# Recurrent scan of a hybrid decoder: sample states read once for both operands, output matmuls in runs of one shape, sample state update by four heads

## The reference, cut to what matters

```python
def _wkv_step(S, inp):
    r_t, w_t, k_t, v_t, a_t, b_t = inp
    sa = jnp.einsum('bhij,bhj->bhi', S, a_t)
    S = S * w_t[:, :, None, :] + sa[..., None] * b_t[:, :, None, :] + v_t[..., None] * k_t[:, :, None, :]
    return S, jnp.einsum('bhij,bhj->bhi', S, r_t)
```

## Time and profile before

| | |
|---|---|
| time, median of 3 runs | 3170.84 us (3169.41 to 3178.54) |
| profiled execution: span from first to last instruction | 3169.1 us |
| PE busy | 2695.0 us (85%), 21151 matmul passes |
| DVE, ACT, POOL busy | 1607.7, 1070.8, 174.8 us |
| first scan, from chunk 1 to the last state update | 258.19 to 455.70 us |
| second scan, the same | 2646.62 to 2839.11 us |

### The profile page before, as it was taken

The page is one execution under the profiler, slowest core; times in us unless marked ns, Lnnn a source line. Parts: engine busy times, 40 slices in busy tenths (PEclk is TensorE's granted clock), DMA queues, the critical chain, the costliest instruction groups (busy, mean ns, idle before and its releaser), DMA issues. The chain is left out here.

```text
span 3169.1 us, 48791 instructions
## 1 busy us (share of the span) xinstructions
PE 2695.0 (85%) x21151; PEld 2385.4 (75%) x21151; DVE 1607.7 (51%) x2358; ACT 1070.8 (34%) x1798; POOL 174.8 (6%) x176
## 2 busy tenths in 40 slices
PE   6939985998847899979989888978997939985999
PEld 5728854998724678869989866678997718864999
DVE  5384336644362577756434843265536374326643
ACT  4333112433311344434334620044434332203442
POOL 0020011000000000000000132200000020011000
PEclk8969867999865899989999965589998978967999
DMA  4210001444200222214434301323442210001442
GB/s 152 90 66 3 6 28 60 153 147 159 98 0 0 67 67 67 67 54 157 149 124 146 138 27 63 131 99 120 147 147 104 83 40 30 6 27 53 147 151 105
DMA packets 44133, 275.70 MB, mean 87 GB/s; under 512 B 5216, under 2 KB 5248, under 8 KB 14096
## 3 DMA queue, kind: packets, MB, share of 16 engines
q1 hardware_dynamic: 43680, 271.95, 24.1%
q0 software_dynamic: 240, 0.64, 0.1%
HBM read 256.32 MB, written 16.24 MB: 86 GB/s over the span
## 5 line engine op out<-in xcount | busy, mean ns | idle before, releaser
L315 PE MATMUL banks<-rounded,rounded 128*128 128x320 f32 x3184 | 1009.8, 317 | 165.3 <-DVE rounded L331 69.1
L316 PE MATMUL banks<-rounded,rounded 128*128 128x320 f32 x3184 | 995.7, 313 | 0.0
L317 PE MATMUL banks<-rounded,rounded 128*128 128x320 f32 x3184 | 995.2, 313 | 0.0
L305 DVE TENSOR_TENSOR rounded<-weight_ring,rounded 128x1024 fp32r<-128x1024 f32 x398 | 487.2, 1228 | 513.4 <-ACT rounded L298 513.1
L315 PEld LDWEIGHTS banks<-rounded,rounded 128*128 128x128 f32 x3184 | 609.4, 191 | 177.3 <-DVE rounded L331 74.3
L316 PEld LDWEIGHTS banks<-rounded,rounded 128*128 128x128 f32 x3184 | 609.7, 191 | 3.6
L317 PEld LDWEIGHTS banks<-rounded,rounded 128*128 128x128 f32 x3184 | 608.8, 191 | 0.0
L298 ACT ACTIVATE rounded<-weight_ring 128x1024 fp32r<-128x1024 f32 x398 | 419.2, 1058 | 414.6 <-PE banks L317 360.1
L942 PE MATMUL banks<-arena 64*64 64x64 f32 x4032 | 146.3, 225 | 22.8 <-PEq L788 20.3
L942 PEld LDWEIGHTS banks<-arena 64*64 64x64 f32 x4032 | 134.4, 140 | 31.0 <-issue 29.2
L470 ACT ACTIVATE arena<-banks 128x320 f32<-128x320 f32 x128 | 56.0, 438 | 247.9 <-PE banks L317 247.9
(11 more groups left out here) (361 smaller groups left out, 3593.1 us busy)
## 6 DMA issues: line engine op xcount, KB each, us to landing
weight_ring<-in_panels SPq DMA_DIRECT2D x206, 1024.0 KB, 4.7
arena<-in_pages SPq DMA_DIRECT2D x64, 320.0 KB, 3.4
arena<-in_ssm SPq DMA_DIRECT2D x8, 1024.0 KB, 4.8
out_ssm_sample<-arena SPq DMA_DIRECT2D x8, 1024.0 KB, 3.8
arena<-in_wkv SPq DMA_DIRECT2D x2, 2048.0 KB, 8.2
out_wkv_sample<-arena SPq DMA_DIRECT2D x2, 2048.0 KB, 6.2
consts<-in_consts SPq DMA_DIRECT2D x1, 1673.5 KB, 9.7
residual<-in_x SPq DMA_DIRECT2D x1, 1280.0 KB, 5.6
```

The lines of the kernel that those rows point to most:

```text
L305: self.k.nc.vector.tensor_tensor(self.k.w_lo[:, i % SPLIT], self.raw(i), self.k.w_hi[:, i % SPLIT].bitcast(F32), ALU.subtract)\
L315: mm(out, hi, x_hi, start=start, stop=False)
L316: mm(out, hi, x_lo, start=False, stop=False)
L317: return mm(out, lo, x_hi, start=False, stop=stop)
```

## The change

It edits `stage_rwkv_scan` alone.

- Sample chunk, xs: a product of a state now takes the sequence's 8 "a" and 8 "r" columns together (16 columns, written as two pieces of 8 with `pair`), and the two heads of a tile f alternate. ACT copies all 512 columns of the bank to `SX`. In x0 and y the state's part is then one product with the unit matrix for each head.
- x0 and y: all products of one kind for eight heads, then all of the other kind, where they took turns by head. Only the first product of a bank half starts with `start`.
- Sample state update: POOL multiplies the end columns by the decay before (`ends`, 16 operations at the start of the stage, read by the sample chunk's transposes) and multiplies SS by the decay when xs has read it (`SSp`, eight operations). The masks are made on DVE by four heads (`masks_of`, eight tensor_scalar of 256 columns each) into two buffers; DVE's multiply behind each add is gone, and so are POOL's masks.

```diff
@@ -908,8 +908,11 @@
-    zmask = [k.at(o, NB, CK), k.at(o + 512, NB, CK)]
+    zm = [k.at(RW["TMP"] + 2048 * i, NB, 4, CK) for i in range(2)]
+    ends = k.at(o, KT, P)
+    SX = [k.at(RW["TMP"] + 16 * P + 1792 * g + 512, 4, P) for g in range(2)]
...
+    pair = lambda a: a.rearrange("p (m t) -> p m t", m=2)
@@ -964,8 +968,11 @@
+                    if smp:
+                        pe.wait_ge(*pool_did.at("ends"))
                     for f in range(4 * g, 4 * g + 4):
-                        ins = nc.tensor.transpose(k.ps[:, 4 * g, (f % 4) * P:(f % 4 + 1) * P], BK[:, f * NCK + c, :], k.const("ident"))
+                        src = ends[:, f, :] if smp else BK[:, f * NCK + c, :]
+                        ins = nc.tensor.transpose(k.ps[:, 4 * g, (f % 4) * P:(f % 4 + 1) * P], src, k.const("ident"))
@@ -1006,10 +1013,11 @@
-                        for h, f, q, r in heads[g]:
+                        for f in range(4 * g, 4 * g + 4):
                             for b in range(NB):
-                                ins = mm(b3(g, 0)[r, q, TS * b:TS * b + TS], SS[r, f * NB + b, :],
-                                         AR[r, f * NCK + c, TS * b:TS * b + TS], start=True, stop=True)
+                                for r in half:
+                                    ins = mm(pair(k.ps[r, 4 * g, (f % 4) * P:(f % 4 + 1) * P])[:, :, TS * b:TS * b + TS], SS[r, f * NB + b, :],
+                                             pair(AR[r, f * NCK + c, :])[:, :, TS * b:TS * b + TS], start=True, stop=True)
                         ins.then_inc(*pe_did.tick("xs", c, g))
@@ -1018,10 +1026,11 @@
                         if smp:
-                            mm(b3(g, 3)[r, q, :], YM[g][r, q, :], eye[r, :], start=True, stop=False)
+                            mm(b3(g, 3)[r, q, :], SX[g][r, q, 0:CK], eye[r, :], start=q == 0, stop=False, skip_group_check=True)
                         elif c:
-                            mm(b3(g, 3)[r, q, :], AR[r, f * NCK + c, 0:CK], S[r, f, :], start=True, stop=False)
-                        ins = mm(b3(g, 3)[r, q, :], att[r, h, 0:CK], z[r, h, :], start=c == 0, stop=True)
+                            mm(b3(g, 3)[r, q, :], AR[r, f * NCK + c, 0:CK], S[r, f, :], start=q == 0, stop=False, skip_group_check=True)
+                    for h, f, q, r in heads[g]:
+                        ins = mm(b3(g, 3)[r, q, :], att[r, h, 0:CK], z[r, h, :], start=c == 0 and q == 0, stop=True, skip_group_check=True)
@@ -1036,24 +1045,22 @@
                     for h, f, q, r in heads[g]:
-                        ins = mm(b3(g, 3)[r, q, :], z[:, h, :], att[:, h, CK:P], start=True, stop=c == 0 or smp)
-                        if smp:
...
+                        ins = mm(b3(g, 3)[r, q, :], z[:, h, :], att[:, h, CK:P], start=q == 0, stop=c == 0, skip_group_check=True)
+                    if c:
+                        for h, f, q, r in heads[g]:
+                            lhs, rhs = (eye[r, :], SX[g][r, q, CK:P]) if smp else (S[r, f, :], AR[r, f * NCK + c, CK:P])
+                            ins = mm(b3(g, 3)[r, q, :], lhs, rhs, start=False, stop=True, skip_group_check=True)
                     ins.then_inc(*pe_did.tick("y", c, g))
...
+            for u in range(4):
+                pe.wait_ge(*vec_did.at("zm", u))
+                for f in (2 * u, 2 * u + 1):
+                    if f >= 4:
                         pe.wait_ge(*vec_did.at("SS", f - 4))
+                    for par in range(2):
+                        ins = mm(k.ps[half[par], f % 4, :], bktok[:, f, half[par]], zm[u % 2][:, :, 2 * (f % 2) + par, :],
+                                 start=True, stop=True)
+                ins.then_inc(*pe_did.tick("dss", u))
@@ -1086,7 +1093,7 @@
-                        s.activation(YM[g], b3(g, 0)[:, 0:4, :], ACT.Copy).then_inc(*act_did.tick("xs", c, g))
+                        s.activation(SX[g].rearrange("p a b -> p (a b)"), k.ps[:, 4 * g, :], ACT.Copy).then_inc(*act_did.tick("xs", c, g))
@@ -1159,27 +1166,38 @@
             vec.wait_ge(*pe_did.at("y", SMP, 1))
...
+            vec.wait_ge(*pool_did.at("SSp"))
+
+            def masks_of(u):
+                if u >= 2:
+                    vec.wait_ge(*pe_did.at("dss", u - 2))
+                for b in range(NB):
+                    ins = v.tensor_scalar(zm[u % 2][:, b, :, :], z[:, 4 * u:4 * u + 4, :], k.const("seq")[:, b:b + 1], None, ALU.mult)
+                ins.then_inc(*vec_did.tick("zm", u))
+
+            masks_of(0)
+            for u in range(4):
+                if u + 1 < 4:
+                    masks_of(u + 1)
+                vec.wait_ge(*pe_did.at("dss", u))
+                for f in (2 * u, 2 * u + 1):
+                    sf = SS[:, f * NB:(f + 1) * NB, :]
+                    v.tensor_tensor(sf, sf, k.ps[:, f % 4, :].rearrange("p (a b) -> p a b", a=NB), ALU.add).then_inc(*vec_did.tick("SS", f))
...
+            for m in range(2):
+                src = BK[:, SMP::NCK, m * CK:(m + 1) * CK].rearrange("p f (b t) -> p f b t", b=NB)
+                dst = ends[:, :, m * CK:(m + 1) * CK].rearrange("p f (b t) -> p f b t", b=NB)
+                for f in range(KT):
+                    ins = nc.gpsimd.tensor_tensor(dst[:, f], src[:, f], bc(pc[:, f, 4:12], TS), ALU.mult)
+            ins.then_inc(*pool_did.tick("ends"))
+            for g in range(2):
+                pool.wait_ge(*pe_did.at("xs", SMP, g))
+                for f in range(4 * g, 4 * g + 4):
+                    sf = SS[:, f * NB:(f + 1) * NB, :]
+                    ins = nc.gpsimd.tensor_tensor(sf, sf, bc(pc[:, f, 4:12], CK), ALU.mult)
+            ins.then_inc(*pool_did.tick("SSp"))
```

More of the change, by code:

```diff
@@ L910, in stage_rwkv_scan @@
         o += 1792
-    zmask = [k.at(o, NB, CK), k.at(o + 512, NB, CK)]
-    assert o + 1024 <= k.arena_size - 104, o
+    assert o <= k.arena_size - 104, o
+    zm = [k.at(RW["TMP"] + 2048 * i, NB, 4, CK) for i in range(2)]
+    ends = k.at(o, KT, P)
+    SX = [k.at(RW["TMP"] + 16 * P + 1792 * g + 512, 4, P) for g in range(2)]
+    assert o + KT * P <= k.arena_size - 104, o
     z = k.normed[:, 0:1024].rearrange("p (a b) -> p a b", a=16)
@@ L1038, in _ @@
                     for h, f, q, r in heads[g]:
-                        ins = mm(b3(g, 3)[r, q, :], z[:, h, :], att[:, h, CK:P], start=True, stop=c == 0 or smp)
-                        if smp:
[L1041 to L1046, removed]
+                        ins = mm(b3(g, 3)[r, q, :], z[:, h, :], att[:, h, CK:P], start=q == 0, stop=c == 0, skip_group_check=True)
[3 more added lines that the diff above has]
+                            ins = mm(b3(g, 3)[r, q, :], lhs, rhs, start=False, stop=True, skip_group_check=True)
                     ins.then_inc(*pe_did.tick("y", c, g))
             pe.wait_ge(*act_did.at("y", SMP, 0))
[L1049 to L1053, removed]
+            for u in range(4):
+                pe.wait_ge(*vec_did.at("zm", u))
+                for f in (2 * u, 2 * u + 1):
+                    if f >= 4:
                         pe.wait_ge(*vec_did.at("SS", f - 4))
-                    mm(k.ps[r, f % 4, :], bktok[:, f, r], zmask[par].rearrange("p a b -> p (a b)"), start=True, stop=True)\
-                        .then_inc(*pe_did.tick("dss", h))
+                    for par in range(2):
+                        ins = mm(k.ps[half[par], f % 4, :], bktok[:, f, half[par]], zm[u % 2][:, :, 2 * (f % 2) + par, :],
+                                 start=True, stop=True)
+                ins.then_inc(*pe_did.tick("dss", u))
         @block.scalar
```

## The result

The changed kernel takes 3034.32 us in the median (3033.08 to 3038.1, 4 runs) where the kernel before, on the same chip, took 3171.61 (3169.41 to 3178.54, 4 runs): a ratio of 0.9564, 95% interval 0.955 to 0.9577. The profiled execution's span went from 3169.1 to 3032.2 us, by 136.9. The forecast was 3041 in a range of 3024 to 3062.

The account below looks back on a forecast made before the run. PE's list was taken to bound a scan until the sample chunk's y ends, with a busy DVE tail behind. Gains summed to 129.8 us, taking the profiled 3169.1 to 3039.3 and the median to 3041; 8-in-10 range 3024 to 3062.

Parts of the forecast that it names:

- prompt, ds and y: Chunks 1 to 3 of both scans: products in runs take 3.64 us for both groups at 2.4 GHz; gain 39.8 us.
- heads at full clock: A prompt head that needn't start at half clock takes 23.86 instead of 26.68 us, once a scan; gain 5.6 us.
- sample head: Sample chunk's head: half of the time lost to half clock comes back; gain 3.2 us.
- xs: Sample chunk: 256 passes of 16 columns, halves in turn, at 0.03 then 0.053 us each, 10.5 us; gain 15.0 us.
- sample y: Sample chunk's y takes 3.3 us a scan instead of 34.27 and 31.79; gain 59.5 us, the largest term.
- tail: Sample state update behind y: masks, adds and PE's last run take 17.5 us a scan; gain 6.7 us.
- Rival 2: In y, adding to what was just written costs the 0.20 us, not the shape; 3093 us, chance 4%.
- rival 1: In xs, products don't overlap and take 24.4 us, 13.9 a scan more; 3069 us, chance 6%.
- the mask's 0.35 us: In the tail, each of DVE's 32 masks of 256 columns takes 0.35 us, 11.2 us together.
- The update of S: DVE's state update behind a prompt group's y hides under PE's products, priced at nothing; uncovered 6 us in all.
- x0's order: x0's products in the prompt have one shape already, so their order is worth nothing.
- the up to 0.8 us that POOL beside DVE might cost: At the stage's start, POOL working beside DVE may cost up to 0.8 us a scan; none was taken.

Follow-up runs that it names:

- a0_changed_again: The changed kernel itself without edits, timed again as yardstick beside two other runs on one chip; 3032.89 us.
- e1: Changed kernel with the prompt chunks' y back in turns by head (128-row, then 64-row product), sample chunk as changed; 3084.35 us.
- e9: Changed kernel with prompt y in turns by head, but second products take all 128 state rows (prompt output wrong); 3033.61 us.
- e4: Changed kernel with y of chunks 1 to 3 in lagged turns, each 64-row product four heads behind its 128-row product; 3053.66 us.
- e7: Changed kernel with both x0 products of a head following each other again; 3032.56 us beside 3032.89 for the unedited kernel.
- e3: Changed kernel with xs head by head, eight products on one half of the partitions and then eight on the other; 3050.22 us.
- e6: Changed kernel with xs products widened to up to 64 columns, surplus written over by later products; 3023.37 us beside 3032.89 unedited.

## Why the prediction was right

By its own terms, from the windows of both scans (before less after, us):

| term | forecast | measured |
|---|---|---|
| prompt, ds and y | 39.8 | 61.64 - 6 x 3.29 = 41.9 |
| heads at full clock | 5.6 | 2 x (26.68 - 23.80) = 5.8 |
| sample head | 3.2 | 25.80 - 2 x 11.35 = 3.1 |
| xs | 15.0 | 35.95 - 10.83 - 9.84 = 15.3 |
| sample y | 59.5 | 66.06 - 2 x 2.63 = 60.8 |
| tail | 6.7 | 41.73 - 16.02 - 14.32 = 11.4 |
| sum | 129.8 | 138.3 |

The sample head took 11.35 us in both scans. The span fell by 136.9; some 2 us were lost between the scans (from the last state update to the second scan's chunk 1, 2193.2 us for 2190.9). They are no part of the change: in a0_changed_again, the same kernel, this stretch took 2190.7.

**The mechanism was right.** Up to the tail a scan was as long as PE's list, and what the list lost the time lost. The turns were paid for by the change of shape: shown by e1 against e9, which differ in nothing else than the rows of one product. Rival 2 falls by e4, e7 and e9. The Trainium skill states this cause (TensorEngine Tiling (Array Packing), Tiling Modes, Key Properties): to change the tiling mode drains the engine, to change only the tile does not. The runs agree that the change is what costs, with 4.70 us for a group at a clock of 0.97 in e1, and 1.45 in e9; what the engine does in that time they do not show.

**xs overlapped**, as the row of L942 said and rival 1 doubted: 0.029 us a load at full clock, on two halves that write one bank. Rival 1's price was too high besides: with a head's products behind one another xs takes 18.13 us (e3), not 24.4, since its 0.06 and 0.108 us a pass came from L1042 and L1019 needs 0.047 and 0.081.

**The tail was the mis-sized term.** It was put at 17.5 us and took 16.02 and 14.32, and this is more than half of the sum's miss. What was wrong in it is the mask's 0.35 us: as the duration of one it was right (347 ns), but back to back they take 0.27, so 32 masks need 8.6 us and not 11.2. The adds' 0.69 us was right in the same way (683 ns), and eight of them need 5.1 us and not 5.5. The second tail even lies under the forecast's lower bound of 15.3 us. A row's mean is how long one lasts; what a run of them takes is busy time over count. In the earlier trace rows the two are the same (3.8 us over 8 are 0.475, 2.3 over 8 are 0.29), so those rows could not show the overlap; another row of the kernel before does, with 0.64 us a piece at a mean of 685 ns:

```profile
L1124 DVE TENSOR_TENSOR arena<-banks,consts 128x512 f32<-128x512 f32 x40 | 25.7, 685 | 2.6 <-PE banks L964 2.6
```

**Smaller ones.** A change of shape cost 0.15 us between runs, where the forecast took the 0.20 that it costs in turns, and sixteen passes without a change take 0.47 us (e9: thirty-two in 0.94, from 280.80 to 281.74), where it took up to 0.52; so ds and y take 3.29 and not 3.64 us. The sample's y ran at full clock. `SSp` had 2.9 us to spare and not 3.7. The update of S was hidden, as no head after a y became longer. x0's order was worth nothing (e7). No row was given for the up to 0.8 us that POOL beside DVE might cost; beside `ends` one DVE operation of a scan took 0.64 us instead of 0.42. Two of the prediction's bounds do not follow from its terms: the low ends of its range add up to 2 x 5.9 = 11.8 us, which gives 3029 and not 3026, and 32 masks of 0.286 us, the adds and PE's last run make a tail of 15.5 us, not 15.3. The result lies inside the range either way.

## What to carry to other kernels

Put PE's products of one tile shape in runs before making any of them fewer: here the order alone gave 71 of 137 us, with every product kept. Where products use half the rows, let the two halves alternate: in xs that made 0.029 us a pass out of 0.047. When work goes to an idle engine, work out how many microseconds ahead of its reader it ends, since that number is where the gain turns into a wait.

## What had not been expected

- At full clock a pass of xs takes the same with 64 columns as with 16: 7.44 us for 256 passes (e6), 0.029 each, and 0.029 in the changed kernel. With 16 the granted clock fell from 1.00 to 0.50 within xs, in both scans and in e3 too; in e6 it stayed at 1.00. Products with up to four times the columns made the kernel faster. What in them the clock answers to was not taken apart.
- A change of shape costs more in turns (0.20 us in e1, 0.21 in e4) than between runs of sixteen passes (0.15). The starts of single passes in the two traces show where the 0.05 us come from. The step across a change is the same in both: 0.15 us from the last pass of one shape to the first of the other (283.04 to 283.19 in the changed kernel, 282.19 to 282.34 in e1), then 0.11 to that head's next pass. But between runs two heads' passes start there 0.007 us apart (three L1052 passes below), and in turns each step has the pass of one head alone.

```profile
283.04 0.22 PE L1048 MATMUL banks<-arena,normed 128*64 128x64 f32 x1
283.19 0.32 PE L1052 MATMUL banks<-arena,normed 64*64 64x64 f32 x3
...
282.19 0.22 PE L1054 MATMUL banks<-arena,normed 128*64 128x64 f32 x1
282.34 0.33 PE L1056 MATMUL banks<-arena,normed 64*64 64x64 f32 x2
```
